# The low parts of the normed rows move from VectorE to GpSimd in a two-layer diffusion block

## The reference, cut to what matters

```
h = rms_norm(x, norm1) * (1 + scale) + shift      # 768 rows x 1024
z = concat(h_context, h_latent) @ w_in            # 1024 x 5824, cut into the inputs of three mixers
```

## Time and profile before

| | us |
|---|---|
| median of 3 timed runs | 2652.72 |
| lowest and highest of them | 2644.62, 2654.12 |
| profiled execution, whole time | 2644.56 |
| its span (first to last instruction) | 2642.8 |
| TensorE (PE) busy in it | 2488.9 |
| VectorE (DVE) busy | 1060.5 |
| ScalarE (ACT) busy | 674.8 |
| GpSimd (POOL) busy | 87.6 |

### The profile page before, as it was taken

The page is one execution under the profiler, slowest core; times in us unless marked ns, Lnnn a source line. Parts: engine busy times, 40 slices in busy tenths (PEclk is TensorE's granted clock), DMA queues, the critical chain, the costliest instruction groups (busy, mean ns, idle before and its releaser), DMA issues. The chain is left out here.

```text
span 2642.8 us, 41041 instructions
## 1 busy us (share of the span) xinstructions
PE 2488.9 (94%) x17564; PEld 1566.6 (59%) x17564; DVE 1060.5 (40%) x2329; ACT 674.8 (26%) x1322; POOL 87.6 (3%) x145
## 2 busy tenths in 40 slices
PE   5999999999899899999999999998999999999998
PEld 3888877777687434443444478876676643343432
DVE  4545354344674313223232564545358431111113
ACT  3621232221543112111121363143236311010101
POOL 1000100000000000000100000100000000000000
PEclk9999999999999899999999999999999999999999
DMA  6111566255641689897989312232216379999996
GB/s 216 57 49 33 143 194 201 66 178 174 213 173 54 263 347 385 309 396 296 378 347 354 141 41 65 65 97 75 72 57 202 135 279 410 409 409 409 409 409 279
DMA packets 241828, 580.72 MB, mean 220 GB/s; under 512 B 11462, under 2 KB 120240, under 8 KB 240624
## 3 DMA queue, kind: packets, MB, share of 16 engines
q1 hardware_dynamic: 232160, 550.21, 56.1%
q0 software_dynamic: 9488, 27.90, 3.3%
HBM read 554.94 MB, written 23.13 MB: 219 GB/s over the span
## 5 line engine op out<-in xcount | busy, mean ns | idle before, releaser
L971 PE MATMUL ps<-h_hi,m_lo 128*128 128x512 f32 (+1 forms) x1152 | 344.3, 370 | 1.7 <-DVE arena L2147 1.7
L1395 PE MATMUL ps<-arena 128*32 128x512 f32 x1740 | 259.2, 593 | 1.6 <-ACT arena L1819 1.1
L1396 PE MATMUL ps<-arena 128*32 128x512 f32 x588 | 258.0, 593 | 0.0
L971 PEld LDWEIGHTS ps<-h_hi,m_lo 128*128 128x128 f32 x1152 | 207.0, 189 | 53.2 <-issue 16.8
L944 PE MATMUL ps<-m_lo,h_hi 128*128 128x256 f32 (+1 forms) x1248 | 233.2, 289 | 5.2 <-DVE m_lo L2120 2.9
L971 PE MATMUL ps<-h_lo,m_lo 128*128 128x512 f32 (+1 forms) x576 | 204.3, 355 | 0.0
L944 PEld LDWEIGHTS ps<-m_lo,h_hi 128*128 128x128 f32 x1248 | 196.1, 194 | 13.7 <-issue 9.7
L1541 PE MATMUL ps<-arena 128*64 128x512 f32 x832 | 187.8, 597 | 11.1 <-DMA arena<-in_moe_w_up 8.5
L944 PE MATMUL ps<-m_lo,h_lo 128*128 128x256 f32 (+1 forms) x624 | 177.3, 284 | 0.0
L1395 PEld LDWEIGHTS ps<-arena 128*32 128x32 f32 x1740 | 70.3, 110 | 164.2 <-issue 160.7
L944 PE MATMUL ps<-h_hi,m_lo 128*128 128x512 f32 (+1 forms) x512 | 141.7, 354 | 7.8 <-DVE h_lo L2225 6.9
(11 more groups left out here) (398 smaller groups left out, 4517.0 us busy)
## 6 DMA issues: line engine op xcount, KB each, us to landing
arena<-in_moe_w_up SPq DMA_DIRECT2D x101, 1024.0 KB, 12.9
arena<-in_moe_w_gate SPq DMA_DIRECT2D x100, 1024.0 KB, 11.7
arena<-in_moe_w_down SPq DMA_DIRECT2D x100, 1024.0 KB, 13.2
ring<-in_w_in SPq DMA_DIRECT2D x42, 1024.0 KB, 5.4
arena<-in_ada_w SPq DMA_DIRECT2D x40, 1024.0 KB, 5.4
oT<-in_moe_w_up SPq DMA_DIRECT2D x27, 1024.0 KB, 14.9
oT<-in_moe_w_down SPq DMA_DIRECT2D x24, 1024.0 KB, 9.1
oT<-in_moe_w_gate SPq DMA_DIRECT2D x16, 1024.0 KB, 9.4
```

The source lines that it names most:

```text
L971: last = mm(to, w[:, k, cols], h[:, k, seg], start=n == 0 and k == 0, stop=n == 2 and k == KD - 1)
L1395: mm(ps[r][32 * b:32 * b + 32, :], c_xg[:, k, j, 32 * b:32 * b + 32], w, start=k == 0, stop=k == KD - 1)
L1396: last = mm(ps[r][96:128, :], c_xg[:, k, j, 32 * r:32 * r + 32], up[:, kk, 512:1024], start=k == 0, stop=k == KD - 1)
```

## The change

The 8 subtractions of each layer leave VectorE's stream and stand in GpSimd's, between the clearing of `w_decay` and the transfers of L856. GpSimd waits before each for both halves of `h_raw`; TensorE waits for `h_lo_ok` as before, which GpSimd now raises. VectorE goes from `h_raw[:, k]` straight to `h_raw[:, k+1]`, or, after slice 3, to the split of the weights.

```
@@ -851,6 +851,9 @@
                 if l:
                     pool.wait_ge(x_ok, before("x_ok", l - 1) + moe_done(l - 1))
                 nc.gpsimd.memset(w_decay[0:2 * RANK, :, :], 0.0).then_inc(gate_zero, 1)
+                for k in range(KD):
+                    pool.wait_ge(h_raw_ok, before("h_raw_ok", l) + 2 * k + 2)
+                    nc.gpsimd.tensor_tensor(h_lo[:, k, :], h_raw[:, k, :], h_hi[:, k, :].bitcast(F32), ALU.subtract).then_inc(h_lo_ok, 1)
                 pool.wait_ge(gate_zero, before("gate_zero", l) + 1)
                 for d, name in enumerate(("gla_w_af", "gla_w_ab")):
                     pool.dma_start(w_decay[RANK * d:RANK * d + RANK, d, :], a[name][l]).then_inc(small_in, 16)
@@ -2221,8 +2224,6 @@
                         dve.wait_ge(h_hi_ok, before("h_hi_ok", l) + 2 * k + i + 1)
                         v.tensor_scalar(h_raw[:, k, seg], bank[:, 0:seg.stop - seg.start], scl[:, 0, k, i:i + 1], modT[l][:, k, i:i + 1],
                                         ALU.mult, ALU.add).then_inc(h_raw_ok, 1)
-                    dve.wait_ge(h_raw_ok, before("h_raw_ok", l) + 2 * k + 2)
-                    v.tensor_tensor(h_lo[:, k, :], h_raw[:, k, :], h_hi[:, k, :].bitcast(F32), ALU.subtract).then_inc(h_lo_ok, 1)
                     if k == 3:
                         chunk_low(l, 1)
```

## The result

| us | before | after |
|---|---|---|
| median of 8 runs | 2644.74 | 2658.01 |
| lowest and highest | 2643.92, 2654.12 | 2653.59, 2660.6 |
| profiled execution, and its span | 2644.56, 2642.8 | 2656.34, 2654.5 |

The ratio of the times is 1.0038, with a 95% interval of 1.0026 to 1.005: slower by 0.38%, some 10 us. (The median of before given ahead of the prediction, 2652.72, was that of three runs.)

The account below looks back on a forecast made before the run. TensorE, busy 94%, was taken to bound the kernel, with a loop over two slices in each stage; 4.7 + 4.6 = 9.3 us on the four runs' mean 2649.0 gave 2658 us, range 2648 to 2668.

Parts of the forecast that it names:

- signs of being wrong: GpSimd instruction under 1.2 or over 2.3 us, slice 3's as short as others, L1079 awaiting w_decay, clock low past slice 2.
- the loop over two slices: Slice k+2 is transposed behind slice k's matmuls; this loop, 5.96 us before, was to become 6.87 us.
- S2 less S0: S0 to S7 are TensorE's starts on the slices; S2 was put 6.87 us after S0 in the second layer.
- G: Price of one subtraction on GpSimd, put at 1.8 us against VectorE's 0.958, with ends 0.82 and 2.9 us.
- G stands four times in this chain: Second layer's chain to S7, by slices 0, 3, 5, 7: 0.1 us more of G adds 0.4 us a stage.
- VectorE goes from L2222 straight to L2120: After slice 3, VectorE passes from scaling (L2222) to the weights' split (L2120) without a semaphore, so starts before GpSimd.
- 2.29 us of hold on S3: VectorE's split holds up GpSimd's subtraction of slice 3 for its whole length, putting S3 at 1529.57 us.
- its rival without a hold: Rival (a): GpSimd and VectorE don't hold each other up; +2.4 us a stage, 2654 us; chance 0.22.
- I count nothing for it: TensorE's slow clock stretch in the first layer moves along with S0, 0.9 us later; no time added.
- Rival (d): Longer idles lower TensorE's clock in the stages: three slow slices each, 1.07 us apiece, 6.4 more, 2665 us; chance 0.10.
- What is pushed back in GpSimd's stream: Three transfers behind the loop issue near S7; w_decay lands 5.9 us after S7, wanted at 7.75, so hidden.
- VectorE's freed time: The 7.7 us a layer freed on VectorE were put at no gain, as it waits for TensorE's transposes through ScalarE.

Follow-up runs that it names:

- experiment 5: Changed kernel with a 768-element GpSimd copy, result unused, ahead of each subtraction; S0 4.0, S4 20.4, S7 32.5 us of the second stage.
- Experiment 3: Kernel before, with only the split of the second weights piece moved from VectorE to GpSimd; second stage: slice 4 at 16.4, slice 7 at 25.2 us.
- experiment 4: Changed kernel with slice 3's subtraction back on VectorE; second stage: slice 4 starts at 17.3 us, slice 7 at 26.9 us.
- 9: Changed kernel with VectorE's split of the second weights piece moved from behind slice 3 to behind slice 7; second stage: slice 7 at 28.6 us.
- experiment 6: Changed kernel with GpSimd made to wait at slice 3 until VectorE has split the weights; second stage: slice 7 starts at 31.3 us.
- experiment 2: Changed kernel with three zero-operand matmuls put before TensorE's wait for slice 4; second stage: slice 7 starts at 28.1 us.
- experiment 8: Kernel before, with VectorE's split of the second weights piece moved from behind slice 3 to behind slice 7; ratio 0.999, second stage 23.0 us.

## Why the prediction came out as it did

The forecast of 2658 us is the measured median, 2658.0, and that is luck. The change was put at 9.3 us and is 10 by the ratio; the level was put at 2649.0, the mean of the four runs shown, and the median of the eight is 2644.7, 4.3 lower. The medians lie 13.3 us apart; the means of the same runs, 2647.1 and 2657.6, lie 10.5 apart, near the ratio's 0.38%. Slower by 0.35%, within 0.5%, had been forecast; measured is 0.38%, with the interval up to that bound. Of the stage's 5.0 us the prediction had 4.7, but two of its own signs of being wrong appeared, one on each side: slice 3's subtraction was as short as the others (1.84 us), and the clock was below full past slice 2. TensorE waited before slices 0, 2, 4, 6 and 7, where 0, 2, 3, 5 and 7 had been named.

- *What bounds the stage.* Right: the loop over two slices. S2 less S0 grew from 5.96 to 6.85 us, predicted 6.87, and experiment 5 moved it by its 0.78.
- *The price.* G was put at 1.8 us, the middle between two and three passes of GpSimd's copy, for which no reason was given but that it lies between; measured 1.795 to 1.845. Experiment 3 gives a second width: 2048 elements in 4.54 us, so 2.1 ns an element and some 0.17 us beside. That is two and a half passes of the copy's 0.84. The Trainium skill, GPSIMD Engine Reference, "Performance versus the Vector engine", with its 1.96 times, would have given 1.88; measured are 1.89 times VectorE's 0.958.
- *How often G counts.* "G stands four times in this chain (slices 0, 3, 5, 7)": four it is, but in other slices. Without hold and clock the stage grows by 2.7 us, three times 0.9 (slices 0, 4 and 6; experiment 4). The chain to S4 goes from S0 by way of slice 1's matmuls and slice 3's scaling to the split behind it, and leaves slice 2's subtraction out; S7 follows S6 at TensorE's pace. The fourth is slice 3, where GpSimd's length counts through the hold on VectorE's split: with the longer step of experiment 5, S4 moved three times 0.78 us and S6 four times.
- *The two engines beside each other.* The mechanism was right and its place wrong; this is the step that failed: "VectorE goes from L2222 straight to L2120". It had to wait for ScalarE's half of the split, L1689, which ends at 1530.92; so GpSimd, started at 1530.04, was first. VectorE's split was recorded with 3.08 us instead of 2.29 and made S4 0.7 us late (18.0, and 17.3 in experiment 4). The prediction had 2.29 us of hold on S3, which made 2.3 of its 4.7 us (its rival without a hold has 2.4); in truth S3 was on pace at 12.8 and S4 late. The trace of before had it: there too ScalarE's half, the row below, ended at 1525.34, only as VectorE came to the split at 1525.37, and VectorE has now come 0.96 us earlier, to wait.

```profile
1523.43 1.91 ACT L1686 ACTIVATE m_lo<-ring 128x2048 fp32r<-128x2048 f32 x1
```

Experiments 3 and 9 show the hold in both directions, and experiment 6 shows what the assumed order costs. The Trainium skill, SBUF — State Buffer, "Who interferes with whom", calls the shared pair of ports an exclusive lock, for which issue order decides who blocks. The traces agree, with 3.16 and 3.78 us.
- *The clock.* "I count nothing for it": wrong. Rival (d), which had three slow slices in each stage, happened with one in each, slice 4: it cost 1.57 us in the second (experiment 2). In the first layer the clock was granted at 0.51 to 0.64 of full speed from 66 to 70 us, and S4 to S7 took 11.22 us. So the stage's 5.0 us are 2.7 for G, 0.7 for the hold, 1.6 for the clock, where 4.7 had been put down to G and a full hold. The near-equal sums hide two errors of 1.6 us each. Over both layers TensorE waits 13.8 us for the moved line, where it waited 6.9; these 6.9 more and the slow slices' 3.1 make about the 10 us.
- *What is pushed back in GpSimd's stream.* Hidden, as predicted, with more to spare. L1082 (L1079 before) runs 7.75 us after S7 (1556.09 less 1548.34), as before. The transfers of L859 (L856 before), issued from 1548.23 on, landed in 1.8 us, where they had taken 5.0 to 5.3:

```profile
DMA to landing us min/median/max: 1.8/1.8/1.9
```

Around their issue the DMA engines' busy share was 0.92 or more before, and is 0.17 or less now.

- *VectorE's freed time.* Worth nothing, as predicted; it is busy 14 us less over the program and the stage is longer.

## What to carry to other kernels

An engine that is idle 97% of the time is no free place for work that a busier one waits on: ask how long the step takes there and in which loop it stands. Before moving work between VectorE and GpSimd, look in the trace for which two-input instructions will meet, and which of the two will be released first; the release may hang on a third engine. When one step of such a loop waits behind an unrelated instruction (here the split, 1.43 us), moving that instruction to where nothing is behind it can gain where moving the step loses (experiment 8: 1.3 us a stage less; the change: 5.0 more). And when a forecast time comes out, look whether its parts did.

## What the runs showed of the hardware

- GpSimd's float32 subtraction from SBUF: 1.81 us at 128x768, 4.54 us at 128x2048.
- With two SBUF inputs each, an instruction of VectorE and one of GpSimd do not run side by side; the later one's record starts on time and grows by nearly the remainder of the other, all but 0.13 to 0.14 us of it (0.96 to 3.16 and 2.29 to 3.08 us on VectorE, 1.8 to 3.78 us on GpSimd). VectorE's scaling from PSUM ran beside GpSimd's subtraction at its usual 1.26 us.
- In the second stages the granted clock fell to 1.2 GHz behind idles of 2.17, 2.41, 2.94 and 3.06 us, each with 1 us or more of idle within the two slices ahead, and in experiment 5 also behind 1.85 us, two slices after the 2.94; it stayed full behind 2.37 us with 0.19 us ahead of it (experiment 3), and behind 1.44 us with 1.08 ahead (experiment 4). What decides it, these runs don't settle: in the first layer the slow stretch at slices 0 and 1, behind 3.40 us of idle, differed from run to run for the same work: S1 at 6.0 us with the clock full (experiment 2), at 7.6 (after) and at 8.4 (experiment 4).
